# Fourier mixing in a two-layer diffusion backbone: sums over 129 of 256 tokens with the rest mirrored, and later waits in the merge

## The reference, cut to what matters

```python
def fourier_mix(pf):
    b, n, _ = pf.shape
    f = pf.reshape(b, n, FOURIER_GROUPS, FOURIER_GROUP_DIM).astype(jnp.float32)
    y = jnp.fft.fft2(f, axes=(1, 3), norm='ortho').real
    return y.reshape(b, n, FOURIER_W).astype(pf.dtype)

def merge_branches(pg, yd, ym, yf, w_bd, w_bm, w_bf, w_o):
    g = jax.nn.sigmoid(pg.reshape(pg.shape[:-1] + (N_BRANCHES, D_MODEL)))
    merged = g[..., 0, :] * (yd @ w_bd) + g[..., 1, :] * (ym @ w_bm) + g[..., 2, :] * (yf @ w_bf)
    return merged @ w_o
```

## Time and profile before

| | us |
|---|---|
| median of 3 runs | 2257.45 |
| lowest and highest run | 2257.26, 2259.85 |
| the profiled execution | 2260.39 |
| its span in the trace | 2258.6 |

### The profile page before, as it was taken

The page is one execution under the profiler, slowest core; times in us unless marked ns, Lnnn a source line. Parts: engine busy times, 40 slices in busy tenths (PEclk is TensorE's granted clock), DMA queues, the critical chain, the costliest instruction groups (busy, mean ns, idle before and its releaser), DMA issues.

```text
span 2258.6 us, 30336 instructions
## 1 busy us (share of the span) xinstructions
PE 2176.7 (96%) x12156; PEld 1892.0 (84%) x12156; DVE 1378.9 (61%) x2328; ACT 860.5 (38%) x1464; POOL 67.9 (3%) x78
## 2 busy tenths in 40 slices
PE   6999999999999999999999999999999988998998
PEld 3887887987888888888888898888888877998998
DVE  5789885565562334567877556686646553556554
ACT  4321222545463223432222252222245553455443
POOL 0000001000000000100000100000010000000001
PEclk9999999999999999999999999999999997999999
DMA  7545543311112222334544323465333121544553
GB/s 276 206 163 182 195 172 126 132 65 41 59 64 81 97 98 80 112 131 140 177 165 159 122 96 140 144 219 195 132 122 127 53 79 43 207 161 174 172 198 117
DMA packets 73132, 306.25 MB, mean 136 GB/s; under 512 B 7456, under 2 KB 13472, under 8 KB 56992
## 3 DMA queue, kind: packets, MB, share of 16 engines
q1 hardware_dynamic: 53984, 236.95, 30.2%
q10 hardware_dynamic: 19008, 67.35, 8.3%
HBM read 299.03 MB, written 5.24 MB: 135 GB/s over the span
## 4 chain that ended last, share of the span: by engine, by line
PE 69%; DVE 3%; ACT 2%; issue 1%; DMA 1%; DVEq 0%; ACTq 0%
PE ps L535 20%; PE ps L536 20%; PE ps L537 20%; PE ps L970 1%; DVE w_lo L1642 1%; PE ps L844 1%; ACT w_hi L1114 1%; PE ps L1010 1%; DMA w_raw<-in_wout 1%; PE ps L821 0%; PE ps L959 0%; PE ps L1019 0%; PE ps L1021 0%; PE ps L852 0%; PE ps L824 0%
## 5 line engine op out<-in xcount | busy, mean ns | idle before, releaser
L535 PE MATMUL ps<-xn_hi,w_hi 128*128 128x512 f32 (+1 forms) x2336 | 822.0, 352 | 23.7 <-DVE xn_lo L1797 7.6
L1114 ACT CAST w_hi<-w_raw 128x1024 fp32r<-128x1024 f32 (+5 forms) x516 | 445.1, 871 | 1042.1 <-PE ps L537 705.2
L1642 DVE TENSOR_TENSOR w_lo<-w_raw,w_hi 128x1024 fp32r<-128x1024 f32 (+5 forms) x516 | 513.1, 1002 | 498.2 <-ACT w_hi L1114 496.1
L537 PE MATMUL ps<-xn_lo,w_hi 128*128 128x512 f32 (+1 forms) x2336 | 812.2, 348 | 0.0
L536 PE MATMUL ps<-xn_hi,w_lo 128*128 128x512 f32 (+1 forms) x2336 | 811.9, 348 | 0.0
L535 PEld LDWEIGHTS ps<-xn_hi,w_hi 128*128 128x128 f32 x2336 | 445.9, 191 | 85.0 <-issue 23.0
L537 PEld LDWEIGHTS ps<-xn_lo,w_hi 128*128 128x128 f32 x2336 | 445.7, 191 | 55.0
L536 PEld LDWEIGHTS ps<-xn_hi,w_lo 128*128 128x128 f32 x2336 | 446.0, 191 | 52.7
L535 PE MATMUL ps<-split_scratch,w_hi 128*128 128x512 f32 (+1 forms) x1036 | 364.0, 351 | 0.6 <-DVE split_scratch L2129 0.6
L536 PE MATMUL ps<-split_scratch,w_lo 128*128 128x512 f32 (+1 forms) x1036 | 361.1, 349 | 0.0
L537 PE MATMUL ps<-split_scratch,w_hi 128*128 128x512 f32 (+1 forms) x1036 | 360.8, 348 | 0.0
(11 more groups left out here) (174 smaller groups left out, 1609.4 us busy)
## 6 DMA issues: line engine op xcount, KB each, us to landing
w_raw<-in_up SPq DMA_DIRECT2D x88, 1024.0 KB, 4.8
ada_w<-in_ada ACTq DMA_DIRECT2D x128, 512.0 KB, 4.4
w_raw<-in_merge SPq DMA_DIRECT2D x48, 768.0 KB, 4.3
w_raw<-in_dn SPq DMA_DIRECT2D x32, 768.0 KB, 4.7
w_raw<-in_dn SPq DMA_DIRECT2D x32, 640.0 KB, 4.2
w_raw<-in_proj SPq DMA_DIRECT2D x20, 1024.0 KB, 4.8
w_raw<-in_wout SPq DMA_DIRECT2D x16, 512.0 KB, 3.6
w_raw<-in_uk SPq DMA_DIRECT2D x16, 384.0 KB, 3.5
```

Source lines behind the costliest of these rows:

```text
L535: nc.tensor.matmul(out, w_hi, hi, start=first, stop=False)
L537: return nc.tensor.matmul(out, w_hi, lo, start=False, stop=last)
L1114: nc.scalar.copy(wh[:, u % 2, h, 0:w], raw[:, u % RAW, h, 0:w]).then_inc(hi_ready, 1)
L1642: nc.vector.tensor_tensor(wl[:, u % 2, h, 0:w], raw[:, u % RAW, h, 0:w], wh[:, u % 2, h, 0:w].bitcast(F32), ALU.subtract).then_inc(split_r ...
```

## The change

The four token sums of a job are now two pairs with results of their own. The sine sums (DFT_S) go into columns 0 to 128 of the bank, the cosine sums (DFT_C) into columns 256 to 384; each matmul has 129 moving columns instead of 256. ScalarE copies the sine part to SBUF (`Sin`), VectorE writes cosine plus sine to tokens 0 to 128 of a float32 tile `Yf` and cosine minus sine, for n from 1 to 127, in falling order to tokens 255 down to 129. ScalarE then rounds from `Yf`, one job later than before, and VectorE subtracts. The bank is free after VectorE's second instruction (`yf_summed`).

In the merge the three waits now stand at the first projection of their own branch, behind that unit's gate product.

```diff
-                            pe.wait_ge(yf_ready, k0 + t - 2)
+                            pe.wait_ge(yf_summed, k0 + t - 2)
...
-                        for tt in range(2):
-                            nc.tensor.matmul(ps[:, 6 + b, 0:SEQ], AB[:, b, tt, 0:P], DFT_C[:, tt, :],
-                                             start=(tt == 0), stop=False)
-                            ins = nc.tensor.matmul(ps[:, 6 + b, 0:SEQ], AB[:, b, tt, P:2 * P], DFT_S[:, tt, :],
-                                                   start=False, stop=(tt == 1))
+                        for n, table in enumerate((DFT_S, DFT_C)):
+                            for tt in range(2):
+                                ins = nc.tensor.matmul(ps[:, 6 + b, SEQ * n:SEQ * n + HALF], AB[:, b, tt, P * (1 - n):P * (2 - n)],
+                                                       table[:, tt, 0:HALF], start=(tt == 0), stop=(tt == 1))
...
-                pe.wait_ge(ydlo_ready, DIFF_HEADS * (l + 1))
-                pe.wait_ge(ymlo_ready, 4 * (l + 1))
-                pe.wait_ge(yf_ready, done["four"])
...
+                        if (i, j) == (0, 0):
+                            pe.wait_ge(ydlo_ready, DIFF_HEADS * (l + 1))
+                        elif (i, j) == (0, 1):
+                            pe.wait_ge(ymlo_ready, 4 * (l + 1))
+                        elif (i, j) == (0, 2):
+                            pe.wait_ge(yf_ready, done["four"])
...
-                        nc.scalar.copy(YFh[:, g, sc_], ps[:, 6 + (t - 1) % 2, 0:SEQ]).then_inc(yf_hi, 1)
+                        if t >= 3:
+                            act.wait_ge(yf_summed, k0 + t - 2)
+                        nc.scalar.copy(Sin[:, (t - 1) % 2, 0:HALF], ps[:, 6 + (t - 1) % 2, 0:HALF]).then_inc(sin_taken, 1)
+                    if t >= 2:
+                        g, sc_ = jobs[t - 2]
+                        act.wait_ge(yf_summed, k0 + t - 1)
+                        nc.scalar.copy(YFh[:, g, sc_], Yf[:, (t - 2) % 3, :]).then_inc(yf_hi, 1)
...
-                    nc.vector.tensor_tensor(YFl[:, g, sc_], ps[:, 6 + t % 2, 0:SEQ], YFh[:, g, sc_].bitcast(F32),
-                                            ALU.subtract).then_inc(yf_ready, 1)
+                        even, odd = ps[:, 6 + t % 2, SEQ:SEQ + HALF], Sin[:, t % 2, 0:HALF]
+                        nc.vector.tensor_tensor(Yf[:, t % 3, 0:HALF], even, odd, ALU.add)
+                        nc.vector.tensor_tensor(Yf[:, t % 3, SEQ - 1:HALF - 1:-1], even[:, 1:HALF - 1], odd[:, 1:HALF - 1],
+                                                ALU.subtract).then_inc(yf_summed, 1)
+                    if t >= 1:
+                        g, sc_ = jobs[t - 1]
+                        dve.wait_ge(yf_hi, done["four"] + t)
+                        nc.vector.tensor_tensor(YFl[:, g, sc_], Yf[:, (t - 1) % 3, :], YFh[:, g, sc_].bitcast(F32),
+                                                ALU.subtract).then_inc(yf_ready, 1)
```

More of the change, by code:

```diff
@@ L50 @@
 F_HALVES = [12, 10]
+HALF = SEQ // 2 + 1
 MODT = N_MOD * DC
@@ L248, in build @@
         DFT_S = v(SD[:, 1536:2048], "p (t n) -> p t n", t=2)
+        Sin = v(SC[:, 0:2 * SEQ], "p (b n) -> p b n", b=2)
+        Yf = v(SC[:, 2 * SEQ:5 * SEQ], "p (b n) -> p b n", b=3)
         Qh, Ql, Kh, Kl = (v(R[:, a:a + 2048], "p (h n) -> p h n", h=4) for a in (0, 2048, 4096, 6144))
@@ L338, in build @@
         yf_done = sem("yf_done")
+        sin_taken = sem("sin_taken")
+        yf_summed = sem("yf_summed")
         yf_hi = sem("yf_hi")
@@ L1523, in _ @@
                 jobs = [(g, sc_) for g in range(FG) for sc_, _ in streams(both)]
-                for t in range(len(jobs) + 1):
+                for t in range(len(jobs) + 2):
                     if t < len(jobs):
@@ L1530, in _ @@
                                        ).then_inc(ab_ready, 1)
-                    if t >= 1:
-                        g, sc_ = jobs[t - 1]
+                    if 1 <= t <= len(jobs):
                         act.wait_ge(yf_done, k0 + t)
-                        nc.scalar.copy(YFh[:, g, sc_], ps[:, 6 + (t - 1) % 2, 0:SEQ]).then_inc(yf_hi, 1)
+                        if t >= 3:
[5 more added lines that the diff above has]
+                        nc.scalar.copy(YFh[:, g, sc_], Yf[:, (t - 2) % 3, :]).then_inc(yf_hi, 1)
                 done["four"] += len(jobs)
@@ L2212, in _ @@
                 jobs = [(g, sc_) for g in range(FG) for sc_, _ in streams(both)]
-                for t, (g, sc_) in enumerate(jobs):
-                    done["four"] += 1
-                    dve.wait_ge(yf_hi, done["four"])
-                    nc.vector.tensor_tensor(YFl[:, g, sc_], ps[:, 6 + t % 2, 0:SEQ], YFh[:, g, sc_].bitcast(F32),
-                                            ALU.subtract).then_inc(yf_ready, 1)
+                for t in range(len(jobs) + 1):
+                    if t < len(jobs):
+                        dve.wait_ge(sin_taken, done["four"] + t + 1)
+                        if t >= 3:
+                            dve.wait_ge(yf_ready, done["four"] + t - 2)
+                        even, odd = ps[:, 6 + t % 2, SEQ:SEQ + HALF], Sin[:, t % 2, 0:HALF]
[7 more added lines that the diff above has]
+                                                ALU.subtract).then_inc(yf_ready, 1)
+                done["four"] += len(jobs)
                 m = M[("merge", l)]
```

## The result

The changed kernel took 2239.73 us (median of 4 runs, 2238.21 to 2243.42) against 2257.36 us of the kernel before: a ratio of 0.9929, with a 95% interval of 0.9909 to 0.9950. The forecast was 2244.7 us with a range of 2241.5 to 2250.

The account below looks back on a forecast made before the run. The prediction took the Fourier stage to be bound by the columns streaming through TensorE. Narrower sums (10.2 us) plus the seam (2.6 us) made 12.8 us, from a median of 2257.45 to 2244.7 us, range 2241.5 to 2250.

Parts of the forecast that it names:

- What bounds the kernel: Fourier stage: bound by the columns streaming through TensorE, busy 96% of the span, so time taken there is not swallowed behind.
- Part 1: Token sums of the Fourier stage: records fall from 0.2155 to 0.109 us, saving 0.85 us a job, 10.2 us over 12.
- Part 2: ScalarE and VectorE in the Fourier stage: their work fits in TensorE's 1.73 us a job, costed at nothing.
- Part 3: Seam from Fourier stage to merge: moved waits remove TensorE idle time of 1.33 and 1.24 us, saving 2.6 us.
- rival 1: Seam to the merge: it closes but TensorE loses the time elsewhere, so only the narrower sums pay, 2247.3 us; 6%.
- The sentence on the clock: Outside the Fourier stage: clock stretches may shift with the earlier timeline, sized at the 2.6 us spread of the runs before.
- hand-overs: ScalarE in the Fourier stage: 0.3 us for each of three instructions makes a job 2.1 us, 2249 us in all; 5%.
- weight loads that do not hide: Token sums: at 129 columns a record stays near 0.2155 us, so only the seam pays, 2254.9 us; 5%.
- the slower one: Fourier stages of both layers: narrow sums run at the lower clock throughout, about 2268 us; 3%.
- The 81 ns of the Trainium skill: Token sums: records even shorter, 0.081 us each, save 15.5 us with the seam, 2242.0 us; a rival at 3%.

Follow-up runs that it names:

- e8: Changed kernel with 65 instead of 129 moving columns in each token sum, the sums of tokens 65 to 128 left out; 2241.9 us in one run.
- e1: Kernel before with only the three merge waits moved, sums still 256 columns wide; 2252.13 us against 2257.26, ratio 0.9973.
- e2: Changed kernel with the three waits put back ahead of the merge, so narrow sums alone; 2250.84 us.
- padded runs: Changed kernel with 19 unread matmuls (8.2 us) between Fourier stage and merge of layer 0; mean 2251.0 us over 17 runs.
- filled kernels: Unread matmuls placed in TensorE's idle times, in the changed kernel (mean 2234.5 us) and in the kernel before (mean 2248.5 us).
- e15: Changed kernel with 19 unread matmuls (8.2 us) between Fourier stage and merge of layer 0; 2250.2 us.
- e6: Changed kernel with 8 unread matmuls (3.45 us) between Fourier stage and merge of layer 0; 2243.87 us.
- e7: Changed kernel with unread 128-column float32 matmuls in five kinds of TensorE idle time; 2233.88 us against 2256.4 for the kernel before, ratio 0.9902.

## Why the prediction was wrong, point by point

- **What bounds the kernel**: right. TensorE bounds the stage before and after; its stream became shorter and no wait behind took the gain.
- **Part 1, the narrower sums**: right in mechanism, 2% off in size. A job takes 1.76 us, not 1.73, and saves 0.83 us, not 0.85. The record next to what is added (L595, 0.106 us) was the right one to take. e8 shows that there is a floor under it that fewer columns do not lower; that the weight load sets it stays the prediction's reading.
- **Part 2, the others keep up**: right. ScalarE's copy took 0.27 us (0.26 forecast), its rounding from SBUF 0.41 (0.37), VectorE's two new instructions 0.29 and 0.28. Writing in falling order costs nothing that can be seen: 127 columns backwards take 0.28 us, 129 forwards 0.29.
- **Part 3, the seam**: right, and slightly small. Both stages with their seams gained 12.5 us in the pair of traces against 12.8 in the sum. e1 shows 1.5 and 1.4 us for the two seams where the sum had 1.33 and 1.24, and e1 and e2 together show that rival 1 (the idle time is not the semaphores') was wrong.
- **The sentence on the clock is the step that failed**: "Clock stretches elsewhere (0.93 in the attention of layer 1) may shift with the earlier timeline; the runs of before spread by 2.6 us, and I take that as their size." It sized the clock's part at nothing in the sum and at 2.6 us around it. Three runs do not show a spread: 62 runs of the same kernel spread by 10.7 us. And the rows had told of the stretches at the lower level (0.93 over 203 us is 28 us at that level). What the runs showed in its place: the changed kernel's runs have a higher mean clock than those of the kernel before (0.9871 against 0.9856), and with it 2.6 us more gain between the means (15.1 against the 12.5 in place); in the pair of traces, with 77 and 54 us at the lower level, 8.2 us lie outside of the change, and one stretch alone cost 3.8 us. With half of the 10.7 us on each side of 2244.7 the range would have begun at 2239.3 and just held the result.
- **Luck**: the four runs of the result lie 1.4 us (median) below the median of all 16. That is luck; without it the time would have stood at the edge of the range, 0.3 us below it instead of 1.8. The gain above the sum did not: it is 2.3 us over all runs, with a standard error of 0.8.
- **The base** was hardly a part of it: the forecast started from 2257.45 us, 0.3 above the median of the 62 runs. But the profiled execution of before (2260.39 us) lay 3.7 us above their mean, and that of the changed kernel (2239.65 us) 2.0 below the mean of its 16, which is why the pair of traces differs by 20.7 us and the means by 15.1.
- The rivals for less gain (hand-overs, weight loads that do not hide) and the slower one (the clock falls in the stage) did not occur: the clock was 1.00 in both stages. The records stand 0.112 us apart. The 81 ns of the Trainium skill ("TensorE: Matmul & The Clock Gate", section "Back-to-back issue gap") is not what these float32 records show.

**What stays open.** Of the 15.1 us that the means differ by, 12.5 are shown in place, in three traces of the changed kernel. The other 2.6 (standard error 0.8) go with the higher granted clock of its runs. That its place in time gives it this clock is likely and not proven: traces of one kernel agree on the stretch behind the wait of 2.07 us while kernels that reach it at other times differ, and the padded runs have the old clock again, but their time (9.4 for 8.2 us) and that of the filled kernels (14.0 for 12.8) lean that way without settling it. Why the clock falls behind such a wait at one time and not at another, no run here shows.

## What to carry to other kernels

Where moving columns are float32 and every matmul has a new 128-column weight, halve the columns down to about 128 and no further: that is where these records met their floor. If results need one more hop through slower engines, let the next stage begin with a product that does not read them. And sum the time at the lower clock as a term of its own, with the spread of many runs of the base around it: the runs of this base differ by 10.7 us, about 0.5%. If every run comes with its granted clock, compare the two kernels at equal clock before you explain a few microseconds; here it took the gain from 15.1 back to the 12.5 us that the traces have in place.

## What the runs showed of the hardware

- Waits of the same length (2.07 and 2.08 us) at the same place of the program were followed by 10 us at 1.2 GHz in the kernel before and in e15, and by none in three traces of the changed kernel, in e1 and in e6. One cannot read from the length of a gap alone whether the clock will fall. The stretch cost 3.8 us.
- 72 useless matmuls of 0.21 us (e7), 15 us of work laid mostly into TensorE's waits, made the kernel 7.4 us faster, and the rows show 2.4 GHz for more of the stages behind (0.97 instead of 0.88 in the 100 us from 1820).
- Float32 records with 4, 65, 129 and 64 and 128 columns stand 0.101 to 0.112 us apart at full clock: with a new weight each, a record of fewer than about 128 columns costs nearly the same as one of 128.
- In 62 runs of one kernel the mean granted clock went from 0.983 to 0.988 and the mean time at each value from 2260.8 to 2252.6 us: about 1.6 us for 0.001 of clock.
